# Second norm by token tile: the first two state input units computed together, tile by tile, the second with a home of its own for its high weight parts

## The reference, cut to what matters

```python
y2 = (jax.nn.silu(f_gate) * f_up) @ w_ffn_out[l]
x = x + rms_norm(y2, g_post_ffn[l])                      # the branch norm, then the sum
...
h = modulate(rmsnorm(x, norm_g[layer]), shift, scale)    # the second norm, "x2"
u, z = jnp.split(h @ w_in, 2, axis=-1)                   # "su" and "sz" units
# S5: per group of 16 channels, 64 complex states
bu = einsum(u, bb)                                       # the input matmuls
x = scan of x[t] = a * x[t-1] + bu[t]
y = einsum(x.re, c_re) - einsum(x.im, c_im) + d * u
y = gelu(y); y = y * sigmoid(y @ w_glu + b_glu)          # the gate units
out = (y * silu(z)) @ w_out
```

## Time and profile before

| | |
|---|---|
| time, three runs | 3051.67, 3051.94, 3053.2 us (median 3051.94) |
| the profiled execution | 3049.54 us, of which the span is 3047.8 us |
| busy: TensorE, VectorE, ScalarE, GpSimd | 3003.5 (99%), 2198.8 (72%), 1486.6 (49%), 354.0 us (12%) |
| weight loads of TensorE | 2545.4 us (84%) |
| mean granted TensorE clock | 0.997 of full speed |
| high parts, L1562 (ScalarE) | 996 x 1058 ns |
| low parts, L2657 (VectorE) | 996 x 1263 ns |
| from memory | 698.92 MB read, 235 GB/s over the span |

### The profile page before, as it was taken

The page is one execution under the profiler, slowest core; times in us unless marked ns, Lnnn a source line. Parts: engine busy times, 40 slices in busy tenths (PEclk is TensorE's granted clock), DMA queues, the critical chain, the costliest instruction groups (busy, mean ns, idle before and its releaser), DMA issues.

```text
span 3047.8 us, 46410 instructions
## 1 busy us (share of the span) xinstructions
PE 3003.5 (99%) x16652; PEld 2545.4 (84%) x16652; DVE 2198.8 (72%) x2686; ACT 1486.6 (49%) x2021; POOL 354.0 (12%) x397
## 2 busy tenths in 40 slices
PE   8999999999999999999999999899999999999998
PEld 8888888888888888888888888799888888888887
DVE  6779888668767766886765765799966758566675
ACT  6455444454444445444444444656544534555653
POOL 0000000015555521551000000000000000000000
PEclk9999999999999999999999999999999999999999
DMA  7668776658888876998888985566555669544444
GB/s 266 215 234 281 249 282 218 198 175 313 306 282 316 313 277 179 296 300 262 294 277 252 276 285 195 154 203 199 178 190 192 240 191 346 195 153 153 157 166 166
DMA packets 272546, 718.20 MB, mean 236 GB/s; under 512 B 27425, under 2 KB 120097, under 8 KB 271073
## 3 DMA queue, kind: packets, MB, share of 16 engines
q1 hardware_dynamic: 251328, 668.23, 65.3%
q10 hardware_dynamic: 13936, 28.69, 2.9%
q0 software_dynamic: 7088, 18.62, 1.7%
HBM read 698.92 MB, written 16.53 MB: 235 GB/s over the span
## 4 chain that ended last, share of the span: by engine, by line
PE 91%; DVE 5%; ACT 2%; issue 1%; DMA 0%; DVEq 0%; ACTq 0%; SPq 0%
PE psum L911 62%; PE psum L848 12%; PE psum L851 6%; PE psum L892 4%; PE psum L972 1%; DVE ring_parts L2657 1%; PE psum L985 1%; PE psum L1051 1%; ACT hi_parts L1562 1%; PE psum L1199 1%; DVE work L2825 0%; PE psum L1059 0%; PE psum L1354 0%; ACT arena_low L2031 0%; PE psum L999 0%
## 5 line engine op out<-in xcount | busy, mean ns | idle before, releaser
L2657 DVE TENSOR_TENSOR ring_parts<-ring,hi_parts 128x1024 fp32r<-128x1024 f32 x996 | 1220.9, 1263 | 371.7 <-ACT hi_parts L1562 367.2
L1562 ACT ACTIVATE hi_parts<-ring 128x1024 fp32r<-128x1024 f32 x996 | 1020.3, 1058 | 620.0 <-DMA ring<-in_stream 419.5
L911 PE MATMUL psum<-hi_parts,arena_low_parts 128*128 128x512 f32 x3408 | 1088.3, 391 | 0.1
L911 PEld LDWEIGHTS psum<-hi_parts,arena_low_parts 128*128 128x128 f32 x3408 | 639.8, 188 | 134.6 <-issue 2.5
L911 PE MATMUL psum<-hi_parts,arena_high_parts 128*128 128x512 f32 x2224 | 730.3, 394 | 1.1 <-DVE arena_high_parts L2381 1.1
L911 PE MATMUL psum<-ring_parts,arena_low_parts 128*128 128x512 f32 x1856 | 722.2, 389 | 0.0
L911 PEld LDWEIGHTS psum<-hi_parts,arena_high_parts 128*128 128x128 f32 x2224 | 417.5, 188 | 92.0 <-issue 5.6
L911 PEld LDWEIGHTS psum<-ring_parts,arena_low_parts 128*128 128x128 f32 x1856 | 348.6, 188 | 71.3
L911 PE MATMUL psum<-ring_parts,arena_high_parts 128*128 128x512 f32 x960 | 373.6, 389 | 0.0
L848 PE MATMUL psum<-arena_low_parts,hi_parts 128*128 128x512 f32 x1024 | 330.9, 399 | 2.7 <-DVE ring_parts L2657 2.7
L892 PE MATMUL psum<-arena_low_parts,hi_parts 128*128 128x256 f32 (+1 forms) x1184 | 232.2, 287 | 2.2 <-DVE ring_parts L2657 1.4
(11 more groups left out here) (433 smaller groups left out, 2674.6 us busy)
## 6 DMA issues: line engine op xcount, KB each, us to landing
ring<-in_stream SPq DMA_DIRECT2D x1270, 512.0 KB, 4.8
ssm_kept<-work POOLq DMA_DIRECT2D x16, 512.0 KB, 6.9
arena_high<-ssm_kept ACTq DMA_DIRECT2D x11, 512.0 KB, 3.6
frac_kept<-work POOLq DMA_DIRECT2D x15, 256.0 KB, 6.2
early<-frac_kept ACTq DMA_DIRECT2D x15, 256.0 KB, 3.1
work<-ssm_kept ACTq DMA_DIRECT2D x5, 512.0 KB, 4.2
arena_high<-in_mem ACTq DMA_DIRECT2D x8, 256.0 KB, 6.8
arena_high<-in_x ACTq DMA_DIRECT2D x1, 2048.0 KB, 12.5
```

What stands on the lines that cost most here:

```text
L911: mm = pe.matmul(stream_bank(b + t), r32(x[part][:, kg * KG + kk, t * P:(t + 1) * P]), r32(cols), start=(kg == 0 and kk == 0 and n == 0), ...
L1562: act.activation(r32(slot_of(hi, g)[:, cols]), ring[:, g % RING, cols], ACT.Copy).then_inc(hi_made, 1)
L2657: dve.tensor_tensor(r32(slot), slot, as32(slot_of(hi, g)[:, cols]), ALU.subtract).then_inc(cut_done, 1)
```

## The change

- `first_states` takes the place of `steps(BEFORE_S5)` and the first two `su` units. TensorE first turns the four groups of tile 0, then multiplies: tile 0, group by group, each with su 0 and su 1; then tile 1, all of su 0, then all of su 1. Each matmul has 128 moving columns (one tile). The turns of tile 1 stand behind groups 2 and 3 of tile 0. `inputs(0)` and `direct_terms(0)` come behind both units.
- The norm goes by tile on ScalarE (`second_norm`, `x2_values`, 128 columns each) and VectorE (`x2_split`, one group of one tile). Tile 0 is scaled before tile 1's sum is whole. A small sine activation stands ahead of the third group's values. `x2_cut` counts the split groups.
- Su 1's high parts go to `work[:, 0:4]`, so that its cut takes its place at the last fo1 unit, ahead of the norm. Su 2's cut comes behind the norm and, on VectorE, ahead of `products(0)`.
- Su 1's result gets the bank `y_bank(-1)` and no longer shares su 0's.

```diff
-HI_HOMES = {POS[("unit", "ff0", 1)]: 48, POS[("unit", "kvn", 1)]: 96}
+WORK_HOME = POS[("unit", "su", 1)]
+HI_HOMES = {POS[("unit", "ff0", 1)]: 48, POS[("unit", "kvn", 1)]: 96, WORK_HOME: None}
...
+            def first_states(x):
+                for turn in NORM_X2[:4]:
+                    side(turn)
+                turns = {(0, 2, 1): NORM_X2[4:6], (0, 3, 0): NORM_X2[6:7], (0, 3, 1): NORM_X2[7:]}
+                banks = [free_bank(su_bank(0)), free_bank(y_bank(-1))]
+                for t in range(TT):
+                    parts = [(group, u) for group in range(KT // 4) for u in range(2)]
+                    for group, u in parts if t == 0 else sorted(parts, key=lambda part: part[1]):
+                        slot = cut_half("su", u, group // 2)
+                        pe.wait_ge(x2_cut, 4 * t + group + 1)
+                        for k in range(4 * group, 4 * group + 4):
+                            cols, tokens_ = slice(k * P, (k + 1) * P), slice(t * P, (t + 1) * P)
+                            for n, (w, part) in enumerate(((hi, 0), (hi, 1), (ring, 0))):
+                                mm = pe.matmul(banks[u][:, tokens_], r32(slot_of(w, slot)[:, cols]), r32(x[part][:, k, tokens_]),
+                                               start=(k == 0 and n == 0), stop=(k == KT - 1 and n == 2))
+                        for turn in turns.get((t, group, u), []):
+                            side(turn)
+                        if t == 1 and group % 2:
+                            release(mm, "su", u, group // 2)
...
             prepare(0)
-            steps(BEFORE_S5)
-            t_unit("su", 0, h3T, own_bank=su_bank(0))
+            first_states(h3T)
             inputs(0)
             direct_terms(0)
-            t_unit("su", 1, h3T, own_bank=su_bank(1))
             prepare(1)
...
+            def second_norm():
+                load_root_table()
+                last_of_fo1(0)
+                branch_root(1, 0)
+                square_of_sum("x2", 0, 0, 0)
+                square_of_sum("x2", 0, 1, 1)
+                last_of_fo1(1)
+                root(NORMS["x2"], 0)
+                branch_root(1, 1)
+                act.wait_ge(mod_gain, 1)
+                x2_values(0)
+                square_of_sum("x2", 1, 0, 2)
+                x2_values(1)
+                square_of_sum("x2", 1, 1, 3)
+                root(NORMS["x2"], 1)
+                did(act.activation(stat[:, 45:46], ones[:, 0:1], ACT.Sin))
+                for j in range(2, len(NORM_X2)):
+                    x2_values(j)
...
+            second_norm()
+            cut(POS[("unit", "su", 0)] + LEAD, halves_=(0,))
             prepared(0)
-            cut(POS[BEHIND_NORM] + LEAD)
             sines(0)
             inputs_turned(0)
             cosines(0)
-            cut(POS[("unit", "su", 0)] + LEAD)
+            cut(POS[("unit", "su", 0)] + LEAD, halves_=(1,))
             direct_block(0)
...
+            both_parts(3, 1)
+            rms_mean("x2", 0)
+            branch_mean(1, 1)
+            rms_root("x2", 0)
+            scale_rows(xr, xn, 0, range(0, 2))
+            branch_factor(1, 1)
+            add_half(1, 0)
+            x2_split(0)
+            scale_rows(xr, xn, 0, range(2, 4))
+            add_half(1, 1)
+            x2_split(1)
+            rms_mean("x2", 1)
+            x2_split(2)
+            rms_root("x2", 1)
+            scale_rows(xr, xn, 1)
+            for j in range(3, len(NORM_X2)):
+                x2_split(j)
...
-            steps(BEFORE_S5)
-            cut(POS[BEHIND_NORM] + LEAD)
-            dve.nop().then_inc(evacuated[y_bank(-1) % 4], 1)
+            cut(POS[("unit", "su", 0)] + LEAD, halves_=(0,))
             modulation(1, "kv_norm", "kv_scale", 0)
             modulation(2, "norm1", "nsa_scale", 1)
...
+            cut(POS[("unit", "su", 0)] + LEAD, halves_=(1,))
             products(0)
-            cut(POS[("unit", "su", 0)] + LEAD)
```

More of the change, by code:

```diff
@@ L259, in between @@
     return out
-NORM_X3 = [("norm", "x3", j) for j in range(KT // 2)]
+NORM_X2, NORM_X3 = ([("norm", tag, j) for j in range(KT // 2)] for tag in ("x2", "x3"))
 X3_TILES = [(t, group) for t in range(TT) for group in range(KT // 4)]
@@ L648, in slot_of @@
         def slot_of(w, g):
+            if w is hi and g == WORK_HOME:
+                return work[:, 0:4, :].rearrange("p b n -> p (b n)")
             if w is hi and g in HI_HOMES:
@@ L853, in wide_unit @@
                         release(mm, phase, u, h)
[L855 to L867, removed]
-                            both, narrow = ((hi, both_parts(x, k), banks[u]), (ring, r32(x[0][:, k, :]), banks[u][:, 0:S]))
-                            order = (both, narrow) if k < KT - 1 else (narrow, both)
-                            for n, (w, moving, bank) in enumerate(order):
-                                mm = pe.matmul(bank, r32(slot_of(w, slots[u])[:, cols]), moving, start=(k == 0 and n == 0),
-                                               stop=(k == KT - 1 and n == 1))
-                            if u == 0 and k % (KT // 2) == KT // 2 - 1:
-                                release(mm, phase, 0, h)
-                mm.then_inc(units_done, 2 * RUN[("unit", phase, 1)])
             def t_unit(phase, u, x, i=None, per=0, uses=0, own_bank=None):
@@ L1317, in steps @@
                         plain_unit(step[1], step[2])
-                    elif step[0] == "norm" and (step[1] in ("x1", "x3") or step[1] in FIRST.values() and step[2] >= TURNS_BEFORE):
+                    elif step[0] == "norm" and (step[1] in ("x1", "x2", "x3") or step[1] in FIRST.values() and step[2] >= TURNS_BEFORE):
                         continue
@@ L1750, in side @@
                         part = side_bank(n)[:, c * S:(c + 1) * S]
[L1751 to L1755 removed]
+                        ins = act.activation(r32(dst[0][:, k, :]), part, ACT.Identity, scale=gain[:, k:k + 1], bias=0.0)
                     ins.then_inc(rounded, 1)
@@ L2123, in rms, with scale_rows @@
                 scale_rows(src, dst, t)
-            def scale_rows(src, dst, t):
-                for c in range(D // CHUNK):
+            def scale_rows(src, dst, t, columns=range(D // CHUNK)):
+                for c in columns:
                     cols = slice(c * CHUNK, (c + 1) * CHUNK)
```

131 lines of the change are left out of this document (53 added, 78 removed).

## The result

| | before | after |
|---|---|---|
| median of six runs each | 3052.07 us | 3078.31 us |
| lowest and highest | 3051.09, 3053.30 | 3064.96, 3079.27 |
| the profiled execution | 3049.54 us, span 3047.8 | 3078.76 us, span 3077.0 |
| mean granted TensorE clock in it | 0.997 | 0.989 |

The changed kernel is slower: the ratio of the runs is 1.0074, with a 95% interval of 1.0064 to 1.0083. Its six executions fall in two groups, which the number can't be read without: four took 3077.89 to 3079.27 us at a mean clock of 0.989, two took 3064.96 and 3066.15 us at 0.994; the ratio is over both, the median and the profile are of the first. I had forecast 3060.7 with a range of 3053.5 to 3066.5. Direction right, size wrong: +26.2 us by the medians where I had +8.7.

The account below looks back on a forecast made before the run. VectorE was taken to bound the state stage: first product 11.0 us later, less 2.3 us of cuts moved ahead, gives +8.7 us. That made 3058.3 for the profiled execution, 3060.7 with its 2.4 us below the median; range 3053.5 to 3066.5.

Parts of the forecast that it names:

- the clock's term: TensorE behind fo1: half clock for 1.5 to 3 us of work's worth, plus 1.0 us, ends 0 and 2.
- The price at full clock: su 0 and su 1: 128-column matmuls 0.115 us each (0.11 to 0.12), the two units 22.1 us instead of 11.5.
- Rival 1: su 0 and su 1: 128-column matmuls run at the plain-f32 rate, 0.22 us; +28 us, 3080; chance 0.16.
- Rival 2: su 0 and su 1: weight load hides, 0.066 to 0.081 us a matmul; 3054.3 to 3055.8 us; chance 0.09.
- rival 4: State stage follows TensorE and 128-column matmuls cost half, so 6.9 us come back; faster, 3045.0 us; chance 0.05.
- The steps of the norm: Second norm on VectorE and ScalarE: group 2 of tile 0 cut at 1951.0 us, last cut at about 1961.2.
- The cover for su 1's cuts: Ahead of the norm: VectorE's 2.98 us idle time hides the cuts, costing nothing; 2.35 us without it.
- VectorE's pace: State stage runs at VectorE's rhythm, 14.36 us a chunk, from its first product to the gate units.
- rival 3: State stage: VectorE isn't the bound and TensorE's own delay counts; +5 us, 3057; chance 0.09.

Follow-up runs that it names:

- a_warm2: Changed kernel plus discarded 512-column matmuls (5, 12 and 5) in all TensorE waits behind fo1; 3056.52 us, ratio 1.0015 to the kernel before.
- a_turns: Changed kernel plus 16 discarded plain-f32 transposes of 128 columns ahead of group 2 of tile 0; 3064.43 us, ratio 1.0040 to the kernel before.
- a_wide: Changed kernel with norm by tile kept, but all eight turns first and su 0 and su 1 at 256 columns; 3055.33 us, ratio 1.0013 to the kernel before.
- b_mid128: Kernel before with su 6, 7 and 8, deep in the chunks, done by token tile at 128 columns; one execution, 3068.56 us.
- b_dve4: Kernel before plus four more VectorE products of 128x1024 in state chunk 5; 3056.44 us, ratio 1.0015.
- b_pe8: Kernel before plus eight discarded 512-column matmuls on TensorE ahead of state chunk 5's gate unit; 3055.02 us, ratio 1.0007.
- b_warm: Kernel before plus discarded 512-column matmuls: 26 ahead of the second norm's first turn, 5 and 10 in the gate units' waits; 3051.22 us, ratio 0.9997.
- a_burst: Changed kernel plus 16 discarded 512-column matmuls ahead of group 2 of tile 0; 3066.32 us, ratio 1.0043 to the kernel before.
- a_warm: Changed kernel plus discarded 512-column matmuls, 5 ahead of the turns and 12 before tile 0's second scaling; four runs 3057.61 to 3060.35 us, five 3073.08 to 3075.05.

## Why the prediction was wrong, point by point

- **The failed step is the clock's term**, "plus 1.0, with 0 and 2 as ends". It measured 21.4 us by the traces and 21.8 by the medians of the changed kernel and a_warm2. I had read from the earlier trace rows when the clock came back, in the third full microsecond of the transposes, and carried it over to other work; at the gate units it took until the sixth, and not even that was an end of my range. And the work of those rows was 16 transposes, and at the gate units matmuls of 512 and 256 columns. After the change it was 8 transposes and then fp32r matmuls of 128 columns, with the 16 transposes of tile 1 among them only in pieces of 8, 4 and 4. Of that kind of matmul I had said that no row showed even the price. An operation that no row shows is unknown in what it does to the clock too, and I had bounded only its duration. The change lets TensorE begin earlier, and so cuts short the transposes behind which the clock used to return: 8 of them in place of 16 between the wait and the first su matmul. That 16 in a row are enough, a_turns and a_wide show.
- **The price at full clock was right.** 0.111 to 0.113 us a matmul (a_warm2, b_mid128) against 0.115 taken and 0.109 from the weight loads. With the clock kept, the product comes 33.03 us behind VectorE's last part of the sum; 35.2 were predicted, 34.2 without the clock's term.
- **Rival 1 gave nearly the right time, 3080, by the wrong mechanism**, which is luck. Its pitch, 0.22, is close to the 0.212 that the changed kernel shows. Only the clock column beside it, and b_mid128, tell that it isn't the operation's price. Rival 2 was wrong (0.113, not 0.066 to 0.081), and rival 4 with it.
- **The steps of the norm held.** Counted from VectorE's last part of the sum, group 2's cut ended at +13.8 (predicted +14.3), behind the table load, which released VectorE after 3.18 us of idling, and the last cut of tile 1 in a_warm2 at +24.2 (predicted +24.5). The cover for su 1's cuts held as well.
- **VectorE's pace held in the two profiles**, which is why 30.4 - 2.15 + 1.31 gives the span's difference. As a rule for all executions it was too strong: rival 3 was set aside on waits at the end of the stage, though the two cadences, 14.36 and 14.51, stand side by side in the trace of before, and b_dve4, b_pe8, b_warm and a_burst each have a stretch at TensorE's. In a_warm2 it held: counted from the last part of the sum, its product is 8.9 us later than before's, and 4.0 us less come behind it (2.8 up to the fifteenth product), 4.9 in all; by the medians it is 4.2 us slower.
- **The chances** gave 0.72 to slower, which it is, but the range ended at 3066.5 because rival 1, with its 0.16, was left out of it. Its pitch came about, by another cause.

## What to carry to other kernels

When a change swaps one kind of matmul for another right behind a wait of TensorE, price it at half clock as well, for its whole length, unless a row shows the clock returning under that very kind; read the granted clock beside every pitch before calling it the operation's cost. Where narrow matmuls must follow a wait, discarded work in that wait can be worth far more than it costs (here 21.8 us), but fill every wait, and no longer than the wait is. Where two engines' cadences are 1% apart, neither is "the bound": take both from the trace. A wait that keeps the clock in one execution and loses it in the next can then decide which of them sets the pace (here 2.5 us), so don't build on one profile.

## What the runs showed of the hardware that I had not expected

- A full clock held through 96 fp32r matmuls of 128 columns in a row (b_mid128, 10.87 us at 1.00), but at 0.50 a stream of 192 of them, with 16 transposes in it, ran for 44 us in the changed kernel's trace without getting it back. The Trainium skill, "TensorE: Matmul & The Clock Gate", section "Part 1: The HAM clock gate (the "warmup" mystery)", says that behind a first stretch of work everything runs at 2.4 GHz. The changed kernel's trace disagrees for this kind of matmul; its two executions at 3065 us may not, as they have no trace.
- Transposes of plain f32 did bring it back (a_turns: 16 of them, 3.43 us, 1.00 from 1962 on; a_wide likewise). The same page, section "Part 4: PE-mode transpose", says that the full clock doesn't engage for transposes. The runs disagree, and the measurement decides.
- One wait of 1.16 us inside the stream cost the clock in five of nine executions of a_warm (about 16 us each by the medians of the two groups), and in none of eleven when filled, as their times and mean clocks have it. A wait of 2.67 us in the kernel before kept the clock in one trace and lost it in another (b_pe8). What in the kind of matmul the chip looks at, the runs don't show.
